# Latent keys of the last chunks loaded features-first, and the first two rounds' loads issued earlier, in a decoder step kernel

## The reference, cut to what matters

```python
def one(args):
    ql, qp, cn, kn, pages = args
    cp = cache_ckv[pages].reshape(-1, KV_LORA)        # 4096 x 256 latents
    kp = cache_kpe[pages].reshape(-1, QK_ROPE_DIM)    # 4096 x 64 rotary keys
    s_past = (einsum('thl,pl->htp', ql, cp) + einsum('thr,pr->htp', qp, kp)) * ATTN_SCALE
    ...
    p = softmax(concatenate([s_past, s_new], axis=-1), axis=-1)
    return einsum('htp,pl->thl', p[..., :n_past], cp) + einsum('hts,sl->thl', p[..., n_past:], cn)
```

## Time and profile before

| | us |
|---|---|
| median of 3 runs | 1326.41 |
| lowest, highest | 1326.16, 1329.97 |
| the profiled execution | 1327.11 |
| its span, first to last instruction | 1325.3 |
| heads of the prompt attention with rounds 0 to 7 | about 709 to 822 |
| tail, rounds 8 to 15, to the last values | about 822 to 896 |

### The profile page before, as it was taken

One profiled execution on the slowest core, in us unless ns is written; L12 is line 12 of the kernel. 1 busy time (PEld: TensorE's weight loads), 2 busy tenths in 40 slices (PEclk: granted clock), 3 DMA queues, 4 the chain that ended last, 5 costly groups with the idle time before them and its releaser, 6 DMA issues.

```text
span 1325.3 us, 27706 instructions
## 1 busy us (share of the span) xinstructions
PE 1298.2 (98%) x11006; PEld 1220.0 (92%) x11006; DVE 783.8 (59%) x1198; ACT 572.2 (43%) x973; POOL 708.9 (53%) x501
## 2 busy tenths in 40 slices
PE   6999999999999999999999999999999999999997
PEld 6877599999999999999998787779999999999997
DVE  6678767646454545467645676665764646454534
ACT  5112365544344434344556454442544444444432
POOL 2322243488887877334344443222358888887731
PEclk9999999999999999999999999999999999999999
DMA  6654337676666333634427889962333233222222
GB/s 237 178 160 146 109 107 183 168 183 180 178 178 180 115 111 111 214 85 140 130 67 290 304 350 382 371 231 77 94 96 96 96 96 96 91 91 89 88 91 68
DMA packets 214417, 207.27 MB, mean 156 GB/s; under 512 B 110417, under 2 KB 196689, under 8 KB 206737
## 3 DMA queue, kind: packets, MB, share of 16 engines
q1 hardware_dynamic: 205552, 149.90, 38.0%
q0 software_dynamic: 8352, 55.05, 10.4%
q10 hardware_dynamic: 384, 0.55, 0.2%
HBM read 190.47 MB, written 31.42 MB: 167 GB/s over the span
## 4 chain that ended last, share of the span: by engine, by line
PE 94%; DMA 3%; ACT 1%; DVE 1%; POOL 1%; issue 0%; SPq 0%; DVEq 0%; ACTq 0%
PE ps L1918 34%; PE ps L2054 22%; PE ps L2042 19%; PE ps L1956 3%; PE ps L2297 2%; PE ps L2186 2%; DMA nat<-cache_ckv,rows 1%; PE ps L2250 1%; PE ps L2237 1%; PE ps L2392 1%; DMA kp<-k_pages 1%; PE ps L1969 1%; PE ps L2227 1%; PE ps L2145 1%; PE ps L2119 1%; PE ps L2307 0%
## 5 line engine op out<-in xcount | busy, mean ns | idle before, releaser
L700 POOL TENSOR_TENSOR wl<-raw,wh 128x512 fp32r<-128x512 f32 (+2 forms) x249 | 432.1, 1737 | 397.8 <-ACT wh L860 397.8
L860 ACT ACTIVATE wh<-raw 128x512 fp32r<-128x512 f32 (+2 forms) x253 | 192.4, 762 | 367.3 <-PE ps L1918 200.2
L1918 PE MATMUL ps<-xh,wh 128*128 128x272 f32 x704 | 148.6, 293 | 11.2 <-DVE xl L1266 10.2
L700 POOL TENSOR_TENSOR wl<-wuv,wh 128x512 fp32r<-128x512 f32 x104 | 134.0, 1299 | 47.5 <-ACT wh L860 47.5
L2054 PE MATMUL ps<-mh,wl 128*128 128x272 f32 x768 | 158.5, 288 | 0.0
L2054 PE MATMUL ps<-ml,wh 128*128 128x272 f32 x768 | 158.3, 288 | 0.0
L2054 PE MATMUL ps<-mh,wh 128*128 128x272 f32 x768 | 158.2, 287 | 0.0
L1918 PE MATMUL ps<-xl,wh 128*128 128x272 f32 x704 | 146.4, 289 | 0.0
L1918 PE MATMUL ps<-xh,wl 128*128 128x272 f32 x704 | 146.0, 289 | 0.0
L1918 PEld LDWEIGHTS ps<-xh,wh 128*128 128x128 f32 x704 | 111.6, 190 | 16.7 <-POOL wl L700 11.4
L2054 PEld LDWEIGHTS ps<-mh,wh 128*128 128x128 f32 x768 | 120.5, 188 | 0.0
(11 more groups left out here) (328 smaller groups left out, 2845.3 us busy)
## 6 DMA issues: line engine op xcount, KB each, us to landing
raw<-w_up SPq DMA_DIRECT2D x32, 1024.0 KB, 5.6
raw<-w_down SPq DMA_DIRECT2D x32, 1024.0 KB, 5.2
k_pages<-cache_kT SPq DMA_DIRECT2D x128, 160.0 KB, 3.5
raw<-k_pages POOLq DMA_DIRECT2D x16, 1024.0 KB, 7.0
raw<-w_pw SPq DMA_DIRECT2D x11, 1024.0 KB, 5.9
shifted<-ext SPq DMA_DIRECT2D x96, 66.5 KB, 2.0
kp<-k_pages POOLq DMA_DIRECT2D x18, 256.0 KB, 8.0
k_pages<-cache_kT SPq DMA_DIRECT2D x128, 32.0 KB, 2.7
```

The lines of the kernel that those rows point to most:

```text
L700: pf.tensor_tensor(weight(wl, u), weight_raw(u), f32(weight(wh, u)), ALU.subtract).then_inc(w_lo, 1)
L860: af.activation(weight(wh, u), weight_raw(u), ACT.Copy).then_inc(w_hi, 1)
L1918: m = tf.matmul(ps[:, bank_of(u) + bank, 0:width], w[:, k, :], a[:, k, part], start=(k == 0 and n == 0), stop=(k == nk - 1 and n == 2))
```

## The change

`LOADED` names six chunks, 25 and 27 to 31, and four things follow.

- Their pages are put in order in full (160 KB instead of 32 KB). Of their 48 pages, 30 are the last page copies, 26 of them in the heads of the prompt attention after round 0.
- `ORDERS` drops their groups from the transposes: rounds 12 and 13 transpose one chunk (four groups) instead of two, rounds 14 and 15 none. ACT's and DVE's copies to `kt` go with them. `latent_scores` reads the loaded chunk of rounds 12 and 13 features-first, and rounds 14 and 15 use `turned_scores`.
- SP loads the six chunks, 1 MB each, with a semaphore `t_late` each: 25 and 27 into the two halves of `raw`, 28 and 29 into new buffers `keys_x` and `keys_pr`, which lie where data is dead by then, all four ahead of the rotary keys of chunk 24; 30 and 31 into `kt`, once the scores of round 13 are out. So `w_o`'s first two blocks wait for the scores of rounds 12 and 13, and the reload of `x` for those of round 14.
- Chunks 0 and 1 are loaded to `early_keys` and a half of `vv` after the third query projection, and chunks 2 and 3 to `raw` where 0 and 1 were. POOL issues no latent loads after round 0.

The diff without the buffer declarations, the semaphores, the same two-line edit in ACT's and DVE's `keys`, and `values`, which now waits for the gather of a chunk that was not transposed:

```diff
@@ -74,6 +73,11 @@
 NAT_SLOT = [j % 4 if j < TURNED else (4, 0, 1, 5, 6, 2, 3)[(j - TURNED) % CB] for j in range(NCH)]
 KEY_SLOT = [j % 2 if j < TURNED + 2 else (2, 3, 4, 5, 6, 0, 1)[(j - TURNED - 2) % CB] for j in range(NCH)]
 PIECES = 1 + 2 * KC
+LOAD_AT = TURNED + 8
+LOADED = (25, 27, 28, 29, 30, 31)
+
+ORDERS = {i: [g for g in (0, 2, 4, 6, 1, 3, 5, 7) if 2 * i + g // 4 not in LOADED] for i in range(NH, NSC)}
+FIRST = {i: sum(len(ORDERS[k]) for k in range(NH, i)) for i in range(NH, NSC + 1)}
 SCALE = float((P + ROPE) ** -0.5)
 BIG, MASKED = 3.0e38, 1.0e35
 RMS_EPS, LN_EPS = 1e-6, 1e-5
@@ -415,7 +425,17 @@
 
         def turned_latents(j, par, c):
             n = (2 * par + c) * PPC * PAGE // 2
-            return f32(raw[:, j % 2, n:n + PPC * PAGE // 2])
+            return turned_buffer(j)[:, n:n + PPC * PAGE // 2]
+
+        def turned_buffer(j):
+
+            if j < 2:
+                return (early_keys[:, :], f32(vv[:, 1, :, :, :].rearrange("p a b c -> p (a b c)")))[j]
+            if j < NCH - 4:
+                return f32(raw[:, (j // 2 + 1) % 2 if j > TURNED else j % 2, :])
+            if j < NCH - 2:
+                return (keys_x, keys_pr)[j % 2][:, :]
+            return kt[:, 4 * (j % 2):4 * (j % 2) + 4, :].rearrange("p g c -> p (g c)")
 
         def page_order(keys_, s):
 
@@ -575,7 +595,7 @@
                 b, p = n // PAGES, n % PAGES
                 page = sp.value_load(pages[b:b + 1, p:p + 1], min_val=0, max_val=cache_kT.shape[0] - 1)
                 j, w = n // PPC, PAGE // 2
-                np_ = PIECES if j < TURNED else 1
+                np_ = PIECES if j < TURNED or j in LOADED else 1
                 sp.dma_start(k_pages[j, :, 0:np_, n % PPC * w:(n % PPC + 1) * w],
                              cache_kT[bass.ds(page, 1), :, 0:np_, :].rearrange("n p e c -> (n p) e c")).then_inc(k_seq[b], 16)
 
@@ -664,13 +684,28 @@
                     sp.wait_ge(ks_mm, i)
                 for n in last_pages[i::NH]:
                     sequence_page(n)
+            def turned_keys(j):
+                sp.wait_ge(k_seq[j // CPS], 16 * PAGES)
+                sp.dma_start(turned_buffer(j), k_pages[j, :, 1:PIECES, :].rearrange("p e c -> p (e c)")).then_inc(t_late[j], 16)
+
             for j in range(TURNED + 2, NCH):
-                if j == NCH - 4:
+                if j == LOAD_AT:
                     sp.wait_ge(ks_mm, NH)
-                    load(units[U_WO].block)
-                    load(units[U_WO].block + 1)
+                    for k in LOADED:
+                        if k < NCH - 4:
+                            turned_keys(k)
+                    turned_keys(NCH - 4)
+                    turned_keys(NCH - 3)
                 rotary_keys(j)
-            sp.wait_ge(sc_mm, 4 * NH)
+            for k in range(2):
+                for j in LOADED:
+                    if j < NCH - 4 and j // 2 % 2 == k:
+                        sp.wait_ge(ks_mm, j // 2 + 1)
+                load(units[U_WO].block + k)
+            sp.wait_ge(ks_mm, NSC - 2)
+            turned_keys(NCH - 2)
+            turned_keys(NCH - 1)
+            sp.wait_ge(ks_mm, NSC - 1)
             sp.dma_start(x[:, 0:3, :], x_keep[:, 0:3, :]).then_inc(x_back[0], 16)
             load(units[U_WO].block + 2)
             sp.wait_ge(e_sum, NB)
@@ -779,13 +814,19 @@
 
             def turned_keys(j):
                 pool.wait_ge(k_seq[j // CPS], 16 * PAGES)
-                pf.dma_start(f32(raw[:, j % 2, :]), k_pages[j, :, 1:PIECES, :].rearrange("p e c -> p (e c)")).then_inc(t_keys[j % 2], 16)
+                pf.dma_start(turned_buffer(j), k_pages[j, :, 1:PIECES, :].rearrange("p e c -> p (e c)")).then_inc(t_keys[j % 2], 16)
 
             for u in range(LD[0] + DC, UK[1]):
                 low(u)
+                if u == PROJ[2]:
+                    pool.wait_ge(x_kept, 16)
+                    turned_keys(0)
+                    turned_keys(1)
             pool.wait_ge(w_lo, PROJ[NH - 1] + 1)
-            turned_keys(0)
-            turned_keys(1)
+            for k in range(2):
+                pool.wait_ge(t_keys[k], 16)
+            turned_keys(2)
+            turned_keys(3)
             pool.wait_ge(freed, units[QR[NH // 2 - 1]].done)
             rotary_keys(0)
             rotary_keys(1)
@@ -806,8 +847,9 @@
                 if (h + 1) // 2 < NH // 2:
                     low(UV[(h + 1) // 2][(h + 1) % 2])
                 pool.wait_ge(ks_mm, h)
-                turned_keys(2 * h)
-                turned_keys(2 * h + 1)
+                if h > 1:
+                    turned_keys(2 * h)
+                    turned_keys(2 * h + 1)
                 rotary_keys(2 * h)
                 rotary_keys(2 * h + 1)
                 if h == NH - 1:
@@ -2174,11 +2220,13 @@
                 if i >= NSC:
                     return
                 for o in groups:
-                    g = ORDER[o]
+                    if o >= len(ORDERS[i]):
+                        return
+                    g = ORDERS[i][o]
                     j, k = 2 * i + g // 4, g % 4
                     if k == 0:
                         pe.wait_ge(c_in[NAT_SLOT[j]], 16 * fills(NAT_SLOT, j))
-                    n = NG * (i - NH) + o
+                    n = FIRST[i] + o
                     if n >= 4:
                         pe.wait_ge((kt_act, kt_dve)[n % 2], (n - 4) // 2 + 1)
                     for q in range(4):
@@ -2228,14 +2276,21 @@
                                   page_order(rotaries(j)[rows_, :], s), start=True, stop=False)
 
             def latent_scores(i, c):
-                b = i // SPB
-                pe.wait_ge(kt_act, 4 * (i - NH) + (2, 4)[c])
-                pe.wait_ge(kt_dve, 4 * (i - NH) + (2, 4)[c])
+                b, last = i // SPB, (FIRST[i] + len(ORDERS[i]) * (c + 1) // KC) // 2
+                pe.wait_ge(kt_act, last)
+                pe.wait_ge(kt_dve, last)
+                if c == 0 and 2 * i + 1 in LOADED:
+                    pe.wait_ge(t_late[2 * i + 1], 16)
                 for par in range(2):
                     for s in range(SETS):
-                        cols = slice((s % 2) * SK // 2, (s % 2 + 1) * SK // 2)
-                        m = tf.matmul(scores_at(i, par)[NS * s:NS * (s + 1)], qs[:, c, b, :], kt[:, ORDER.index(4 * (s // 2) + 2 * par + c), cols],
-                                      start=False, stop=(c == KC - 1))
+                        j, g = 2 * i + s // 2, 4 * (s // 2) + 2 * par + c
+                        out, q = scores_at(i, par)[NS * s:NS * (s + 1)], qs[:, c, b, :]
+                        if j in LOADED:
+                            m = tf.matmul(out.rearrange("p (q g s) -> p q g s", q=2, s=ROWS), q, page_order(turned_latents(j, par, c), s),
+                                          start=False, stop=(c == KC - 1))
+                        else:
+                            cols = slice((s % 2) * SK // 2, (s % 2 + 1) * SK // 2)
+                            m = tf.matmul(out, q, kt[:, ORDERS[i].index(g), cols], start=False, stop=(c == KC - 1))
                 if c == KC - 1:
                     m.then_inc(ks_mm, 1)
 
@@ -2243,7 +2298,10 @@
                 b = i // SPB
                 rotary_scores(i)
                 for k in range(2):
-                    pe.wait_ge(t_keys[k], 16 * (i + 1))
+                    if i < NH:
+                        pe.wait_ge(t_keys[k], 16 * (i + 1))
+                    else:
+                        pe.wait_ge(t_late[2 * i + k], 16)
                 for c in range(KC):
                     for par in range(2):
                         for s in range(SETS):
@@ -2345,9 +2403,12 @@
             pe.wait_ge(pv_lo, NH)
             keys(NH, range(3, 8))
             for i in range(NH, NSC):
-                rotary_scores(i)
-                for c in range(KC):
-                    latent_scores(i, c)
+                if len(ORDERS[i]) > 0:
+                    rotary_scores(i)
+                    for c in range(KC):
+                        latent_scores(i, c)
+                else:
+                    turned_scores(i)
                 values(i - 1)
                 keys(i + 1, range(5))
                 if i == NSC - 1:
```

21 lines of the change are left out of this document (15 added, 6 removed).

## The result

| | before | after |
|---|---|---|
| median | 1326.87 us | 1336.85 us |
| lowest, highest of 4 runs | 1326.16, 1329.97 | 1335.35, 1337.50 |
| profiled execution, its span | 1327.11, 1325.3 | 1336.92, 1335.0 |

The ratio is 1.0069, 95% interval 1.0051 to 1.0087: the changed kernel is some 9.2 us (0.69%) slower. It is the ratio of the means; the medians lie 10.0 us apart. The prediction, 1328.4 with a range up to 1335.0, was wrong: it had put 0.34 on slower, and none of its cases reached this far.

The account below looks back on a forecast made before the run. PE sets the pace with the DMA engines level; the changed tail was taken as DMA-bound. Heads +1.2 us (-1.1 + 2.3) and tail +0.6 us make about +2 us, 1328.4 by the median; range 1320.5 to 1335.

Parts of the forecast that it names:

- PE's side of the transposes: Tail: transposes fall from 256 rows to 160, taking 11 to 12 us off their busy time.
- the wait of round 1: Heads, round 1: PE's 0.63 us wait for rotary keys goes and the scores shorten, together 1.1 us.
- The two loads put into the projections cost POOL two DMA issues: Query projections: the moved loads cost POOL issues of some 0.6 us each, where POOL and DMA are half idle.
- The page copies: Heads: 26 copies grow by 128 KB, delaying rotary keys in rounds 2, 3 and 7, +2.3 us in all.
- latent scores of round 15 wait for `kt` from DMA for 5 us or more, with DMA share near 1.0 up to then: Tail's end: the sign that would show the main forecast, DMA-bound and level with before, to be right.
- all of it ahead of the latent scores of round 15: Tail from 814.4: 29.0 to 30.0 MB at 409 GB/s must pass before round 15, which starts at 885.8 to 888.2.
- early waits are no loss where the end is bound by the volume: Tail, transposes of rounds 10 and 11: argument against the slow-queue rival, that their waits for gathers cost nothing.
- a sum, used as support only: Round 13's scores to round 15: PE has about 8.5 us of work, the queues 3.1 MB plus 2.1 MB of gathers.
- The tail's queue is slower than its best stretch: Rival, tail: at 382 GB/s round 15 starts 3.6 to 6.2 us later, kernel at 1331 to 1334; chance 0.14.
- waits for `nat`: Tail, rounds 8 to 11: waits of several us, the sign of the slow-queue rival, with round 15 over 4 us later.
- The loads hide: Rival, tail: loads hide and PE sets the pace; full gain -12.0 us, 1314.4, or about 1320; chance 0.20.
- The page copies delay each head: Rival, rotary scores of rounds 2 to 7: copies cost 6.8 us from three rounds, kernel at 1333 to 1334.5; chance 0.18.

Follow-up runs that it names:

- e1: Kernel before with only the early loads of the first two rounds' keys (chunks 0 to 3); 1330.05 us, ratio 1.0016.
- e5: e1 plus one GpSimd wait: the third head's low weight parts are made only after VectorE normalised head 0's rows; 1324.63 us, 0.9981 of the kernel before.
- e9: Changed kernel in full plus the GpSimd wait of e5; 1332.52 us, 1.0033 of the kernel before.
- e2: Kernel before with only the six chunks' page copies made in full (160 KB instead of 32 KB), added bytes unread; 1328.77 us, 1.0004.
- e4: Changed kernel with ScalarE's split of `w_o` one round later, behind round 14's exponential; 1336.78 us, 1.0060 of the kernel before.
- e3: Changed kernel without its early loads, the six tail chunks still loaded; 1333.34 us, 1.0041 of the kernel before.
- e13: e3 with each of the six loads bringing half its chunk, the loaded half read twice; 1328.74 us, 1.0004 of the kernel before.
- e16: e9 with only chunks 28 to 31 loaded late, so `w_o`'s buffers are free earlier; 1330.45 us, 1.0026 of the kernel before.
- e12: Early loads with GpSimd's wait and two late chunks, with those loads, `w_o`'s loads and ScalarE's split made later; 1333.74 us, 1.0041 of the kernel before.
- e17: e16 with the loads of chunks 28 and 29 issued two rotary loads later; 1329.61 us, 1.0017 of the kernel before.
- e10: e5 plus the late part with four chunks (25, 27, 28, 29); 1327.37 us, 0.9999 of the kernel before.
- e14: e9 with e4's order and SyncE issuing chunk 31's keys, a `w_o` block, chunk 30's keys, the second block; 1328.85 us, 1.0010 of the kernel before.
- e8: e3 with e4's ScalarE order and SyncE issuing chunk 31's and 30's keys ahead of `w_o`'s first two blocks; 1330.76 us, 1.0028 of the kernel before.

## Why the prediction was wrong

**PE's side of the transposes: right.** 256 to 160 instructions and 11.7 us, predicted 11 to 12. So was the wait of round 1: it is gone in e1, e5 and the changed kernel, and in e5's trace round 1 comes 0.7 us sooner behind round 0 than before, round 7 1.2 us, predicted 1.1.

**"The two loads put into the projections cost POOL two DMA issues": the step that failed first.** It looked at what the moved issues cost where they arrive. What they had held up where they left wasn't asked: GpSimd's next subtractions came 1.2 us earlier against VectorE's normalisations in head 0 and fell on them, a wait of 2.74 us for TensorE. e5 undoes it with one wait: +0.16% becomes -0.19%; e9 does in the changed kernel, +0.69% becomes +0.33%. That was about half of the loss, and no case of the prediction had it.

**The page copies: too much.** +2.3 us and a rival of 6.8; e2 bounds all of it, clock included, at -0.06% to +0.15%, which is -0.8 to +2.0 us. The scores of rounds 5 to 7 took 1.24, 1.26 and 1.14 us in the changed kernel's trace and 0.66, 0.86 and 1.16 in e4's, which has the same heads (round 7 comes 101.5 us behind round 0, 103.8 there), so most of their stretching is of the execution.

**The tail: the wait was there as told, but the sum that sized it was the wrong one.** That "latent scores of round 15 wait for `kt` from DMA for 5 us or more, with DMA share near 1.0 up to then" came true: 3.12 us behind 5.02, 7.71 in e4, 8.01 in e3. The stretch was 3.2 us longer than forecast. The rate was right (408 GB/s over 818.2 to 894.7), the volume wasn't: 31.2 MB there against 29.0 to 30.0. But the failed step is "all of it ahead of the latent scores of round 15", all bytes over the best rate from 814.4 on, whatever TensorE does: e13 took out 3.1 MB, 7.7 us by that sum, and won 4.6. With it falls "early waits are no loss where the end is bound by the volume". The last two loads are released by the scores of round 13, so what TensorE waits for before, it waits for them too.

Cut there, the stretch from round 7's rotary scores has two parts. To the end of round 13's scores it took 60.6 us before, and 8 groups and the wait for chunk 25 fewer should leave 56.3; the changed kernel took 61.0, and 3.4 of the 4.7 us between are waits for gathers (5.0 us in all). e3 took 62.4, with as much waiting and 1.7 us more by the clock. From there to round 15's latent scores it was 15.1 us before, 18.6 in the changed kernel and 17.7 in e3. For this second part the prediction had a sum, used as support only: 8.5 us of TensorE (9.7 in e3) and 3.1 + 2.1 MB in the queues, 12.7 us, so a wait of 4.2 us. The second load to `kt` took 16.2 us in e3. By itself this sum would have put round 15 at 876.3 + 4.2 = 880.5, further off than the forecast, since it leaves out what the gathers cost before.

**What follows the tail: missing.** +2.2 us: behind the waits TensorE ran at the lower of its two clock levels, 32 latent scores in 3.64 us in place of 1.86. Every step of the prediction assumed that a wait costs its own length.

**The rivals.** "The tail's queue is slower than its best stretch" came nearest in time (1331 to 1334) by another mechanism: the rate was at its best. Its waits for `nat` were there, 1 to 2.4 us each. "The loads hide" and "The page copies delay each head" fell.

**Open.** What puts e16's keys at 12.4 to 15.1 us isn't taken apart: gathers, `x` and the rest of `w_o` were there together, and no run took them one by one. A buffer for chunks 30 and 31 that is free before round 13 wasn't tried. The 16.2 us of e3 against 12.7 by bytes aren't taken apart either. Nor was the changed kernel's loss of 0.36% in head 0 accounted for beyond 3.3 us, if there is more to it.

## What to carry to other kernels

Before moving an instruction off an engine's queue, look at what stands behind it and what it will then run beside; a DMA issue can be the spacer that keeps GpSimd off VectorE. Where a load is released by the consumer's own progress, sum the bytes in the queues between the release and the need, and add what delays the release, in place of summing the whole stage; even so the sum was 3.5 us short here. And before mending the longest wait in a trace, ask what would end the next one: in e4 a wait of 5.02 us was worth nothing.

## What the runs showed of the hardware

- A VectorE scaling from SBUF to SBUF stands still beside GpSimd's subtractions: in e1 one of 128x384 took 2.61 us, through two back-to-back (all four normalisations took 1.36 without them); in e12 two of 32x2 numbers took 2.25 and 2.31 us, one through each subtraction of 2.4 us (four together 0.9 without them). GpSimd's load issues beside the same instructions cost nothing (1.36 us).
- A short wait can have a second price. Behind waits of 1.74 (e17), 1.85 (e3) and 2.27 us (e2) 24 transposes took 4.5 us, the clock at 0.57 to 0.60 over the 4 us; behind 1.61 (before), 1.78 (e5), 2.05 (e16) and 2.11 us (e10) they took 2.84 at full clock. So the length of the last wait doesn't tell which. Behind 6 to 9 us the 32 latent scores took 3.4 to 3.6 us in place of 1.86.
- The 16 DMA engines held 404 to 408 GB/s over 76 to 80 us with gathers and loads mixed; in such a stretch a 1 MB load took from 7.2 us (chunk 31's keys in e14) to 25.6 us (chunk 29's keys in the changed kernel) to land. With two blocks of `w_o` issued ahead of them the loads to `kt` took 14.3 and 16.2 us (e3), with the blocks issued behind them 8.0 and 9.5 us (e8), and with them issued 8 us earlier 12.4 and 15.1 us (e16).
